# Second layer's branch stage: gate and value tiles as three-pass products, convolution and recurrence started from the first channel pairs

## The reference

```
proj = h @ w_in                        # 2048 -> 2*1024 (conv) + 1024 (ssm) + 2*2048 (gates)
glu  = a[:1024] * sigmoid(a[1024:])
y    = depthwise causal conv, 31 taps, over glu, + bias
branch_conv = silu(layernorm(y)) @ conv_w_out
states = associative scan of a complex diagonal recurrence driven by ssm_in
z    = gelu(C @ states + d_skip * ssm_in)
branch_ssm = (z @ w_val) * sigmoid(z @ w_gate)
gates = sigmoid(gate_in + b_gate)      # two gates of width 2048
x = x + (gates[0] * branch_conv + gates[1] * branch_ssm) @ w_out
```

## Time and profile before

| what | value |
|---|---|
| median of 3 runs | 2590.22 us (2590.07 to 2593.99) |
| profiled execution | 2592.09 us |
| its span in the profile | 2590.3 us |
| PE busy | 1811.4 us, 70% of the span |
| DVE busy | 1725.9 us, 67% |
| ACT busy | 459.2 us |
| POOL busy | 869.0 us |

### The profile page before, as it was taken

How to read it: one execution, slowest core, us unless ns; L and a number is a source line. 1 busy time by engine, 2 the same in 40 slices (tenths; PEclk the granted TensorE clock), 3 DMA queues, 4 the chain that set the end, 5 groups by cost and what they waited for, 6 DMA issues and landing times. The chain is left out here.

```text
span 2590.3 us, 24148 instructions
## 1 busy us (share of the span) xinstructions
PE 1811.4 (70%) x9470; PEld 1412.1 (55%) x9470; DVE 1725.9 (67%) x2348; ACT 459.2 (18%) x735; POOL 869.0 (34%) x525
## 2 busy tenths in 40 slices
PE   8999999999999999999980000777770000077776
PEld 7999999988888888899860000322220000032222
DVE  6656676423919567254699998777559999844444
ACT  4345555411020101233100000100000000000000
POOL 0000000000000000000147888555658888855552
PEclk9999999999999999999995555999995555599999
DMA  7655555655545554465999999999999999999997
GB/s 199 181 165 163 167 167 151 171 147 140 150 133 157 143 150 144 136 191 150 303 362 391 422 421 422 421 421 422 421 422 422 422 422 422 422 422 422 421 421 311
DMA packets 458287, 747.31 MB, mean 289 GB/s; under 512 B 22130, under 2 KB 391236, under 8 KB 392260
## 3 DMA queue, kind: packets, MB, share of 16 engines
q0 software_dynamic: 73728, 536.90, 50.0%
q1 hardware_dynamic: 383776, 208.68, 28.9%
q10 hardware_dynamic: 676, 0.24, 0.0%
HBM read 743.68 MB, written 2.10 MB: 288 GB/s over the span
## 5 line engine op out<-in xcount | busy, mean ns | idle before, releaser
L452 PE MATMUL ps<-operand,weight_raw 128*128 128x256 f32 x3072 | 668.2, 379 | 1.1 <-DVE operand L1047 0.5
L452 PEld LDWEIGHTS ps<-operand,weight_raw 128*128 128x128 f32 x3072 | 581.9, 190 | 83.2 <-issue 3.7
L718 PE MATMUL ps<-weight_raw,residual_t 128*128 128x512 f32 x368 | 174.1, 618 | 323.9 <-ACT residual_t L995 267.8
L470 PE MATMUL ps<-operand_high,weight_high 128*128 128x256 f32 x1504 | 375.4, 290 | 3.1 <-DVE operand_low L1293 3.1
L404 POOL IOTA slots<- 128x16 f32 x1 | 0.1, 145 | 1103.7 <-DVE operand L1424 1103.7
L471 PE MATMUL ps<-operand_low,weight_high 128*128 128x256 f32 x1504 | 366.9, 284 | 0.0
L718 PE MATMUL ps<-rows_high,residual_t 128*128 128x512 f32 x192 | 90.3, 614 | 346.7 <-ACT residual_t L995 317.4
L1036 DVE TENSOR_TENSOR weight_low<-weight_raw,weight_high 128x2048 fp32r<-128x2048 f32 x94 | 215.4, 2292 | 144.2 <-ACT weight_high L732 143.7
L718 PEld LDWEIGHTS ps<-weight_raw,residual_t 128*128 128x128 f32 x368 | 68.5, 195 | 429.5 <-ACT residual_t L995 329.2
L470 PEld LDWEIGHTS ps<-operand_high,weight_high 128*128 128x128 f32 x1504 | 289.6, 193 | 6.3 <-issue 5.5
L471 PEld LDWEIGHTS ps<-operand_low,weight_high 128*128 128x128 f32 x1504 | 289.9, 193 | 2.6 <-issue 2.2
(11 more groups left out here) (220 smaller groups left out, 2228.5 us busy)
## 6 DMA issues: line engine op xcount, KB each, us to landing
weight_raw<-in_w_in SPq DMA_DIRECT2D x120, 1024.0 KB, 6.2
weight_raw<-in_w_out SPq DMA_DIRECT2D x32, 1024.0 KB, 5.9
weight_raw<-in_peer_w_q SPq DMA_DIRECT2D x16, 1024.0 KB, 10.1
weight_raw<-in_ssm_w_val SPq DMA_DIRECT2D x8, 1024.0 KB, 5.3
weight_raw<-in_ssm_w_gate SPq DMA_DIRECT2D x8, 1024.0 KB, 5.3
weight_raw<-in_conv_w_out SPq DMA_DIRECT2D x8, 1024.0 KB, 5.3
work<-in_x SPq DMA_DIRECT2D x2, 1024.0 KB, 6.3
out_y<-work SPq DMA_DIRECT2D x4, 512.0 KB, 5.3
```

What stands on the lines that cost most here:

```text
L452: mm = nc.tensor.matmul(ps_p[:, t % PSLOTS, :], w[:, k, :], operand[:, k, :], start=(k == order[0]), stop=(k == order[-1]))
L470: nc.tensor.matmul(out, high[:, k, :], o_high[:, k, :], start=(k == order[0]), stop=False)
L718: mm = nc.tensor.matmul(ps_v[:, c, :], diag[:, i // 2 % 16, :], rows[b][:, c * 512:(c + 1) * 512], start=False, stop=False, skip_group_che ...
```

## The change

1. The 24 tiles that feed convolution and recurrence come in a new order, `BRANCH`: values and sigmoids of channel pairs 0 and 1, recurrence inputs 0 to 3, then the pairs 2 to 7, then recurrence inputs 4 to 7. They stay plain.
2. The 32 gate tiles and the 16 slabs (32 half tiles) of the values become split products: 48 more slabs through `split_high` and `split_low`. The operands are split too: the normed input (16 tiles) and z (8 tiles).
3. The convolution's output tiles (plain) now stand ahead of the values. Each is multiplied by its gate out of PSUM (`gate_conv`), which frees the bank.
4. DVE's order is written anew. Convolution of pairs 0 and 1 one by one, `scan(0)`, then convolutions of two channel tiles at a time with a `split_low` behind every fourth tap, `skip_sum(0)` after the first of them; then `scan(1)` with 9 `split_low`, centring and scaling of the layer norm, and 13 `gate_conv` between its steps. The convolution has no padded copy and no loop: tap by tap on shortened ranges.
5. `ssm_outputs(0)` stands behind gate tile 1, `ssm_outputs(1)` behind convolution output tile 13, both into other PSUM banks.

The core of the diff:

```diff
+BRANCH = [("glu", 0), ("sig", 0), ("glu", 1), ("sig", 1), *(("ssm", n) for n in range(4)),
+          *((kind, n) for n in range(2, 8) for kind in ("glu", "sig")), *(("ssm", n) for n in range(4, 8))]
+SSM_OUT, SSM_IN, SSM_GELU, SSM_OUT_CV = 1, 9, 10, 13
+LOW_BESIDE = (1, 2, 3, 4, 6, 7, 8, 9, 11)
...
-            for t in range(8, 56):
-                tile(TILE_IN2, t, op_a)
...
+            for t in range(len(BRANCH)):
+                tile(TILE_IN2, t, normed_in, ready=(lambda k: (h_scaled, KD + k + 1)) if t == 0 else None)
+                if first <= t < first + 4:
+                    ssm_inputs(t - first)
...
+            for t in range(32):
+                split_product(SPLIT_GATE + t, ready=(lambda k: O_GATE + k + 1) if t == 0 else None)
+                if t == SSM_OUT:
+                    pe.wait_ge(bu_freed, 16)
                     ssm_outputs(0)
...
             for t in range(16):
-                tile(TILE_CV, t, op_b[:, KH:KD, :], ready=(lambda k: (conv_act, k + 1)) if t == 0 else None)
+                tile(TILE_CV, t, slots[:, CONV0:CONV0 + KH, :], ready=(lambda k: (conv_act, k + 1)) if t == 0 else None)
+                if t == SSM_OUT_CV:
+                    pe.wait_ge(rooted, 14)
+                    ssm_outputs(1)
...
+            for i in range(16):
+                for m in range(2):
+                    split_product(SPLIT_VG + i, m, KH, ready=(lambda k: O_Z + k + 1) if i == m == 0 else None)
...
+                if t >= len(BRANCH) - 2:
+                    split_high(SPLIT_GATE + t - (len(BRANCH) - 2))
...
                 for j in range(1, CHUNK):
                     rotate(xs[:, j], xs[:, j - 1], 0, CHUNKS)
+                    if half == 1:
+                        beside_scan(j)
...
                 for j in range(CHUNK - 1):
                     rotate(xs[:, j, :, :, 1:CHUNKS], last[:, :, :, 0:CHUNKS - 1], j, CHUNKS - 1)
+                    if half == 0 and j == 11:
+                        split_low(SPLIT_GATE)
+                    if half == 1:
+                        beside_carry(j)
...
+            def conv(first, count, low):
...
+                for lag in range(TAPS2):
+                    for n in range(first, first + count):
+                        own.wait(count - 1)
...
+                            own.step(v.scalar_tensor_tensor(out=y[:, lag:T], in0=u[:, 0:T - lag], scalar=w, in1=y[:, lag:T],
+                                                            op0=ALU.mult, op1=ALU.add))
+                    if low is not None and lag % 4 == 3:
+                        split_low(SPLIT_GATE + low + lag // 4)
...
+            def gate_conv(n):
+
                 dve.wait_ge(proj_done, TILE_CV + n + 1)
                 v.tensor_tensor(slot(GA0 + n), slot(GA0 + n), ps_p[:, n % PSLOTS, :], ALU.mult).then_inc(proj_freed, 1)
...
+            def beside_carry(j):
+
+                if 1 <= j < CHUNK - 2:
+                    gate_conv(j - 1)
+                if j == 7:
+                    for a in range(4):
+                        operand_low(O_Z + a + 1, slot(SSM0 + a), a)
...
+            conv(0, 1, None)
+            conv(1, 1, None)
+            scan(0)
+            split_low(SPLIT_GATE + 1)
+            conv(2, 2, 2)
+            skip_sum(0)
+            conv(4, 2, 9)
+            conv(6, 2, 16)
+            v.tensor_copy(small[:, 43:44], small[:, 0:1]).then_inc(conv_done, 1)
+            scan(1)
+            gate_conv(13)
+            split_low(SPLIT_VG)
+            skip_sum(1)
```

More of the change, by code:

```diff
@@ L193, in build @@
         normed_in = slots[:, 24:40, :]
+        ln_rstd = norm_ws[:, 256:512]
         def slot(s, n=1):
@@ L601, in _ @@
             pe.wait_ge(proj_freed, freed(TILE_IN2))
-            for t in range(8):
-                tile(TILE_IN2, t, op_a, ready=(lambda k: (h_scaled, KD + k + 1)) if t == 0 else None)
             def ssm_inputs(a):
+                pe.wait_ge(proj_freed, freed(TILE_IN2 + BRANCH.index(("ssm", a)) + 1))
+                if a == 4:
+                    pe.wait_ge(ssm_sum, 4)
                 for c in range(2):
@@ L888, in _ @@
             root(12, 1, D, summed=acc_summed)
-            for t in range(8):
-                read_out(TILE_IN2, t, slot(SSM0 + t))
+            for k in range(KD):
+                act.wait_ge(h_scaled, KD + k + 1)
+                act_copy(o_high[:, k, :], normed_in[:, k, :]).then_inc(o_high_ready, 1)
             def ssm_inputs(a):
@@ new lines, in z_high @@
+            def z_high(a):
+                act.wait_ge(z_ready, a + 1)
+                act_copy(o_high[:, a, :], slot(SSM0 + a)).then_inc(o_high_ready, 1)
+            first = BRANCH.index(("ssm", 0)) + 1
+            for t, (kind, n) in enumerate(BRANCH):
+                read_out(TILE_IN2, t, slot(BRANCH_SLOT[kind] + n), ACT.Sigmoid if kind == "sig" else ACT.Copy)
+                if first <= t < first + 4:
+                    ssm_inputs(t - first)
+                if t >= len(BRANCH) - 2:
+                    split_high(SPLIT_GATE + t - (len(BRANCH) - 2))
@@ new lines, in _, with merged_high @@
+            for a in range(4, 8):
+                ssm_gelu(a)
+                z_high(a)
+            def merged_high(n):
+                act.wait_ge(merged, n + 1)
+                act_copy(o_high[:, (n + KH) % KD, :], slot(GA0 + n)).then_inc(o_high_ready, 1)
+            for t in range(32):
+                u, m = t // 4, t % 4
+                if m == 0 and u >= 4:
+                    act.wait_ge(val_gated, u - 3)
+                read_out(TILE_VG, t, slot(val(u) + m), ACT.Copy if m < 2 else ACT.Sigmoid)
+                if t % 2 == 1:
+                    split_high(SPLIT_VG + t // 2 + 2)
+                if m == 3 and 1 <= u < 5:
+                    merged_high(2 * u - 2)
+                    merged_high(2 * u - 1)
@@ L955, in keys_out @@
+            act.wait_ge(proj_done, TILE_OUT2)
+            for n in range(KH, KD):
+                merged_high(n)
             def keys_out(u):
@@ L1377, in taps @@
-            def taps(first, last):
-                with own.loop(first, last, KH) as tap:
-                    for n in range(KH):
-                        own.wait(KH - 1)
-                        own.step(v.scalar_tensor_tensor(out=slot(CONV0 + n), in0=glu_pad[:, n, bass.ds(tap, T)],
-                                                        scalar=params[:, bass.ds(tap * KH + (C_TAP + n), 1)], in1=slot(CONV0 + n),
-                                                        op0=ALU.mult, op1=ALU.add))
@@ new lines, in _ @@
+            scan(1)
+            gate_conv(13)
+            split_low(SPLIT_VG)
+            skip_sum(1)
+            gate_conv(14)
+            gate_conv(15)
+            for a in range(4, 8):
+                operand_low(O_Z + a + 1, slot(SSM0 + a), a)
+            split_low(SPLIT_VG + 1)
+            for u in range(8):
+                split_low(SPLIT_VG + 2 * u + 2)
+                gate_values(u)
+                split_low(SPLIT_VG + 2 * u + 3)
+                if 1 <= u < 5:
+                    merged_low(2 * u - 2)
+                    merged_low(2 * u - 1)
@@ L1433, in _ @@
+            for n in range(KH, KD):
+                merged_low(n)
             add_residual(TILE_OUT2, SPLIT_OUT2, 56)
```

271 lines of the change are left out of this document (125 added, 146 removed).

## The result

| what | before | after |
|---|---|---|
| median | 2591.57 us (4 runs, 2590.07 to 2593.99) | 2562.95 us (4 runs, 2561.14 to 2563.80) |
| ratio | | 0.9887, 95% interval 0.9872 to 0.9902 |
| profiled execution, its span | 2592.09, 2590.3 us | 2563.80, 2562.0 us |

The change gains 28.6 us, 1.1%. The prediction was 2561, with a range of 2549 to 2577, and named a gain of 29.1. It counted from 2590.2, the median of three runs; from the 2591.57 of four runs the same gain leads to 2562.5.

What follows compares the result with a forecast made beforehand. PE was taken to bound the stage, DVE having some 260 us of room. 55.0 saved, less 17.6, 1.3, 2.4, 2.0, 3.3 and 1.4, plus 2.3, gives 29.3; the walk's 29.1 off 2590.2 gives 2561, range 2549 to 2577.

Steps and rivals of the forecast that it cites:

- `skip_sum(0)` costs PE: At gate tile 9, DVE's 11.8 us stretch with `skip_sum(0)` was to cost PE 1.3 us.
- The gain of 55 us: 32 gate and 16 value slabs become split products, each 1.15 us cheaper on PE: 55.0 us less PE work.
- The pause, the largest term against: After two output tiles of the convolution, PE stands for 17.6 us until DVE's first `gate_conv` frees a bank.
- The wait inside the first scan: The `split_low` after carry step 11 waits for ACT; DVE stands from 689 to 705.0 us, about 16 us.
- The clock: Behind PE's pause at the convolution's output, the restart at a lower clock was to cost 2.0 us.
- The join to `w_out_2`: First tile of `w_out_2` takes 9.9 us instead of 6.6, 3.3 more, as half its operand is split late.
- The two bank joins: A term of 1.4 us taken off the gain at two bank joins.
- Carried to the end one for one: The tail follows the second projection by a fixed chain, so the stage's gain reaches the end in full.
- 1 (taps one after the other): In the pairs' convolutions, taps of two tiles run serially, 14 us more: 2575; chance 0.13.
- Rival 2: PE stands for less than 17.6 us at the convolution's output: floor 2542, middle 2550; chance 0.12.
- Rival 3: PE stays at 1.2 GHz to the end of the convolution's output, 48 us more instead of 2: 2607; chance 0.03.
- Rival 4: Value slabs of two half tiles cost as much split as plain, 18 us of gain missing: 2579; chance 0.06.

Runs made afterwards that it cites:

- Experiment 5: The changed kernel with the 32 half tiles of the values plain again and z not split: 2581.45 us.
- experiment 6: The changed kernel with the 32 gate tiles plain again and no split in the convolutions and scans: 2577.46 us.
- Experiment 2: The changed kernel with no split in the first scan, fewer in the pairs, 14 in the second scan, norm sums and first `gate_conv` earlier: 2545.62 us.
- experiment 1: The changed kernel with no split in the first scan; splits 0 to 8 moved into and behind the first pair's convolution: 2562.59 us.
- experiment 8: The changed kernel with 64 unused matmuls put in PE's pause behind the convolution's second output tile: 2562.39 us.
- experiment 3: The changed kernel with five `gate_conv` moved in front of the second scan's carry steps: 2558.72 us.
- experiment 4: The changed kernel with each tap of the three pairs waiting for the one before it instead of the one but one: 2572.50 us.
- experiment 7: The changed kernel with the split of `w_out_2`'s second slab moved behind the last eight operand splits on DVE and ACT: 2560.47 us.
- experiment 9: The changed kernel with the edits of experiment 2 and experiment 7 together: 2541.56 us.

## Why the prediction was right, step by step

The predicted times count on the clock of the trace before; the stage starts 1.07 us later in the trace after, which the last column takes off.

| step | predicted | measured | less 1.07 |
|---|---|---|---|
| first scan starts | 607.8 | 609.03 | 607.96 |
| DVE waits for ACT in it | 16 | 15.77 | |
| first scan ends | 714.9 | 715.73 | 714.66 |
| split and eight taps | 5.35 | 727.00 - 721.68 = 5.32 | |
| `skip_sum(0)` costs PE | 1.3 | 0 | |
| convolution ends | 848.1 | 847.34 | 846.27 |
| PE waits for split 31 | 2.4 | 1.57 | |
| first `gate_conv` ends the pause | 938.9 | 937.33 | 936.26 |
| pause | 17.6 | 17.05 | |
| clock after it | 2.0 | 2.9 | |
| values start | 993.9 | 993.12 | 992.05 |
| values take | 92.2 | 92.89 | |
| first tile of `w_out_2` | 9.9 | 1095.39 - 1086.01 = 9.38 | |
| second tile starts | 1096.0 | 1095.39 | 1094.32 |

- **The gain of 55 us.** PE's busy time fell by 53.1. Experiment 5 confirms the values' part, 18.4. The gates' part shows whole on PE: in the window from 709 to 850 us it does not wait at all, and with plain gates (experiment 6) the first output tile starts 34.9 us later in the stage, 36.4 with the 1.57 us wait that after has there. The two make 54.8.
- **The pause, the largest term against.** Right in place, cause and size. Experiment 2 removes it by changing what stands ahead of it, experiment 6 by removing the splits, which names them as the cause.
- **The wait inside the first scan.** Right in size, and it costs nothing (experiment 1). The prediction said that the head start is given away there. More exactly, it would have been given away a little later too, since the splits follow PE.
- **`skip_sum(0)`: wrong by 1.3 us.** The walk gave the stretch of DVE with it 11.8 us from split to split. DVE's timeline has 10.52, and its four sums take 2.31 of them; below, the two splits, and PE's low pass that needs the second:

```profile
757.04 2.29 DVE L1084 TENSOR_TENSOR weight_low<-weight_raw,weight_high 128x2048 fp32r<-128x2048 f32 x1 [0.51 <-ACT weight_high L766]
...
767.56 2.28 DVE L1084 TENSOR_TENSOR weight_low<-weight_raw,weight_high 128x2048 fp32r<-128x2048 f32 x1
...
769.90 0.39 PE L499 MATMUL ps<-operand_high,weight_low 128*128 128x256 f32 x1
```

The split ends at 769.84, PE asks at 769.90: it just fits.
- **The clock: too small by 0.9 us.** I took 2.0 between the 1.6 and 2.5 of the earlier trace rows; experiment 8 gives 2.9, and experiment 3 the same after a shorter pause. The term scatters: from the restart to `ssm_outputs(1)` PE takes 41.61 us with the clock kept, and 44.52 (after), 43.88, 43.37, 44.44 and 44.54 (experiments 1, 4, 5 and 7) behind a pause of 17.05 or 17.06 us each time. That is a cost of 1.8 to 2.9 us.
- **The second scan.** The walk was 2.6 us late at the first `gate_conv`: the convolution ended 1.8 us sooner, and the scan took 0.8 less.
- **The join to `w_out_2`: 0.5 us too long, in part by luck.** The walk has no clock loss there, and after had none. Seven of the other kernels have the same wait of 2.61 to 2.63 us in that tile, and they lost 0.8 to 1.4 us of clock behind it.
- **Small terms.** The two bank joins cost 0.56 and 0.51 us, 1.1 together, where the sum has 1.4. With the measured terms the sum is 54.8 less 17.05, 1.57, 2.9, 2.8 and 1.1, 29.4 us; the stage gained 30.8. So 1.4 us are left for the small waits of the old order, which the sum put at 2.3; no row shows that term by itself.
- **Slips in writing.** 24 tiles of 6.91 us are 165.8 us and not 165.7, and 48 x 1.15 is 55.2; the items of the join add up to 9.75 and not 9.9; DVE's work adds up to 435 us and not 440, and the stage it stands in is some 557 us long by the walk, not 530. None of them moves the forecast by more than 0.2 us.
- **Carried to the end one for one.** The stage's 30.8 us became 28.3 of span: 1.07 was there at its start, and the part behind it took 1.5 us more. The walk gave the stage 29.1. That the forecast of the whole came within 0.5 us is luck: the stage gained 1.7 us more than forecast, and 2.5 us were lost outside it. What was right on its merits is the price of the products and the place, cause and size of the pause.

Of the rivals, 1 (taps one after the other) is excluded by the eight taps in 3.21 us, and experiment 4 shows that it would have cost 9.6 us. Rival 2 (a shorter wait) is not what the change did; its floor of 2542 is reached by experiment 9 (2541.56), which also shortens the join, and not quite by experiment 2 (2545.62). Rival 3, the clock that stays low for the rest of the output tiles, did not happen: over 940 to 945 us the granted clock was 0.68, a mean of time at both levels, and the twelve tiles lost 2.9 us, not 48. Rival 4 fell with experiment 5.

Experiments 5 and 6 give 18.5 and 14.5 us, 33.0 together, where the change gives 28.6. If they add, the new order without any split product would be some 4 us slower than before, which the longer join (2.8) and the bank joins (1.1) would explain. That kernel was not run, so it stays open.

## What to carry to other kernels

Here inserts in one engine's list (the splits on DVE) may only come at the pace of another engine (PE). In such a list look at the sum of the waits up to the instruction that the other engine stands for, and not at one wait. Taking out a 16 us wait changed nothing, because nine others grew by as much. Spreading the same 32 inserts more thinly over the convolution and more densely over the scan cut the sum of waits from 30.4 to 13.6 us, and with the first release one step forward it gave 17 us. Price a cheaper product at the busy engine's saving less the pause that its extra work on the other engines brings: 37 us of PE were worth 14.5 with the splits in a poor order. Then walk both lists with measured distances from start to start; sums of busy time could not have shown this pause.

## What was not expected of the hardware

- **Distance between dependent and independent DVE operations.** Taps of about 0.475 us start 0.39 us apart (eight in 3.12 us from start to start) when they alternate between two tiles and each waits for the last but one. They start 0.50 apart when each waits for the one before it (eight in 3.99 us, experiment 4); on one tile alone three take 1.52 us. Two alternating tiles are as good as the eight of the kernel before, 0.398 apart. The Trainium skill (VectorE: DVE Perf Modes, "The DRAIN you can't avoid") says that the next operation starts only when the pipe is empty, and adds: "A next op that is not held starts earlier", where a held one waits until every earlier one has finished. The rows of the alternating tiles agree with the addition and not with the first sentence; only where each tap waits for the one before it is the distance the full duration.
- **The clock after a short pause.** 9.25 us of idle time cost 2.9 us of clock, 17.05 us cost 1.8 to 2.9, and with matmuls in the pause the clock stayed at 1.00. In `w_out_2`'s first tile a wait of 2.61 to 2.63 us cost nothing in after, where the granted clock stayed at 1.00 and the tile took 9.38 us. In the other seven kernels with that wait the tile took 10.15 to 10.76 us, 0.8 to 1.4 more; in experiment 2, for one, the rest of that pass took 3.45 us (1071.29 to 1074.74) instead of 2.68 (1090.80 to 1093.48), at a granted clock of 0.66 over 1070 to 1075 us. What decides between the two was not tried.
